# The modulation products beside the heads of three attentions, on GpSimd instead of VectorE

## The reference

```python
def ada_params(c, w, b):
    mod = jax.nn.silu(c) @ w + b
    shift, scale, gate = jnp.split(mod, 3, axis=-1)

def modulated_residual(x, c, g, w_mod, b_mod, fn):
    shift, scale, gate = ada_params(c, w_mod, b_mod)
    h = rms_norm(x, g) * (1 + scale) + shift
    return x + gate * fn(h)
```

## Time and profile before

| | |
|---|---|
| median of 3 runs | 2230.7 us (2225.03 to 2233.52) |
| profiled execution, its time | 2235.24 us |
| profiled execution, its span | 2233.4 us |
| granted TensorE clock, mean | 0.916 |
| TensorE busy | 1965.2 us, 88% |
| VectorE busy | 1664.8 us, 75% |
| ScalarE busy | 1143.7 us, 51% |
| GpSimd busy | 36.5 us, 2% |
| products L1370 | 192, 243.9 us, 1280 ns each |

### The profile page before, as it was taken

How to read it: one execution, slowest core, us unless ns; L and a number is a source line. 1 busy time by engine, 2 the same in 40 slices (tenths; PEclk the granted TensorE clock), 3 DMA queues, 4 the chain that set the end, 5 groups by cost and what they waited for, 6 DMA issues and landing times.

```text
span 2233.4 us, 29567 instructions
## 1 busy us (share of the span) xinstructions
PE 1965.2 (88%) x9224; PEld 1633.4 (73%) x9224; DVE 1664.8 (75%) x2294; ACT 1143.7 (51%) x1600; POOL 36.5 (2%) x47
## 2 busy tenths in 40 slices
PE   2968999877799999999999999585779998678998
PEld 2956887656678888888888888564768877466886
DVE  7877666967498989898898989675676668566554
ACT  2434444333277777777777777424344443434443
POOL 2000000000000000000000000000000000000000
PEclk9988999876699999999999999786689998679999
DMA  7965873964189999999999999373457866435662
GB/s 266 363 204 187 263 250 121 335 201 164 57 287 339 368 337 364 336 350 354 340 362 338 366 337 368 134 248 91 134 178 260 261 209 207 112 112 160 216 208 85
DMA packets 368358, 551.03 MB, mean 247 GB/s; under 512 B 35715, under 2 KB 292998, under 8 KB 368230
## 3 DMA queue, kind: packets, MB, share of 16 engines
q1 hardware_dynamic: 353120, 542.56, 71.9%
q10 hardware_dynamic: 14278, 6.70, 2.2%
q0 software_dynamic: 832, 0.30, 0.1%
HBM read 548.38 MB, written 1.08 MB: 246 GB/s over the span
## 4 chain that ended last, share of the span: by engine, by line
PE 75%; DVE 14%; DMA 5%; issue 3%; ACT 2%; SPq 0%; ACTq 0%; POOL 0%; DVEq 0%; POOLq 0%
PE ps L381 21%; PE ps L383 21%; PE ps L382 21%; PE ps L773 2%; DVE mod_acc L1370 2%; PE ps L919 2%; DVE units_low L376 2%; DMA raw_units<-in_w_in 1%; PE ps L827 1%; PE ps L762 1%; PE ps L750 1%; DMA raw_units<-in_attn_w_qkv 1%; DVE x_tokens L1396 1%; DMA raw_units<-in_conv_w_in 1%; DVE x_normed L1395 1%
## 5 line engine op out<-in xcount | busy, mean ns | idle before, releaser
L376 DVE TENSOR_TENSOR units_low<-raw_units,units_high 128x1024 fp32r<-128x1024 f32 (+2 forms) x840 | 983.5, 1219 | 213.1 <-ACT units_high L372 207.7
L372 ACT ACTIVATE units_high<-raw_units 128x1024 fp32r<-128x1024 f32 (+2 forms) x840 | 845.3, 1057 | 355.0 <-PE ps L383 230.4
L381 PE MATMUL ps<-units_high,hT_high 128*128 128x512 f32 (+2 forms) x1592 | 636.5, 400 | 70.4 <-DVE units_low L376 30.1
L382 PE MATMUL ps<-units_low,hT_high 128*128 128x512 f32 (+2 forms) x1592 | 631.6, 397 | 0.0
L383 PE MATMUL ps<-units_high,hT_low 128*128 128x512 f32 (+2 forms) x1592 | 631.3, 397 | 0.0
L381 PEld LDWEIGHTS ps<-units_high,hT_high 128*128 128x128 f32 (+1 forms) x1592 | 306.4, 192 | 141.0 <-issue 38.1
L383 PEld LDWEIGHTS ps<-units_high,hT_low 128*128 128x128 f32 (+1 forms) x1592 | 305.3, 192 | 67.2
L382 PEld LDWEIGHTS ps<-units_low,hT_high 128*128 128x128 f32 (+1 forms) x1592 | 306.0, 192 | 65.9
L381 PE MATMUL ps<-units_high,aT_high 128*128 128x512 f32 x616 | 252.5, 410 | 0.0
L1370 DVE SCALAR_TENSOR_TENSOR mod_acc<-mod_in,silu_c,mod_acc 128x1024 f32<-128x1024 f32 x192 | 243.9, 1280 | 6.2 <-DMA mod_in<-in_mod_w 3.2
L382 PE MATMUL ps<-units_low,aT_high 128*128 128x512 f32 x616 | 242.9, 394 | 0.0
(11 more groups left out here) (229 smaller groups left out, 1570.0 us busy)
## 6 DMA issues: line engine op xcount, KB each, us to landing
raw_units<-in_moe_w_gate SPq DMA_DIRECT2D x352, 256.0 KB, 4.4
raw_units<-in_moe_w_up SPq DMA_DIRECT2D x352, 256.0 KB, 5.6
raw_units<-in_moe_w_down SPq DMA_DIRECT2D x176, 512.0 KB, 6.1
mod_in<-in_mod_w SPq DMA_DIRECT2D x96, 512.0 KB, 5.8
mod_in<-in_w_mod SPq DMA_DIRECT2D x96, 512.0 KB, 5.5
raw_units<-in_w_gu SPq DMA_DIRECT2D x176, 256.0 KB, 3.3
raw_units<-in_w_down SPq DMA_DIRECT2D x44, 512.0 KB, 4.1
raw_units<-in_w_in SPq DMA_DIRECT2D x32, 512.0 KB, 8.5
```

The costliest lines, as they stand in the source:

```text
L372: eng.activation(whi[:rows, n % H, 0:width], raw[:rows, n % R, 0:width], ACT.Copy).then_inc(f.hi, 1)
L376: eng.tensor_tensor(low[:rows, n % R, 0:width], raw[:rows, n % R, 0:width], whi[:rows, n % H, 0:width].bitcast(F32), ALU.subtract).then_in ...
L381: pe.matmul(dst, ah, bh, start=start, stop=False, **kw)
L382: pe.matmul(dst, ah, bl, start=False, stop=False, **kw)
```

## The change

The products are taken out of `beside_heads`, and GpSimd does them: for each, `tensor_scalar` scales the piece in its slot, GpSimd waits for that on a semaphore of its own, and `tensor_tensor` adds it to `mod_acc`. They stand in GpSimd's program for m = 4, 5 and 7 between the bias row of the columns and the memset of the gate's part. VectorE skips these numbers of `MOD_ORDER`, and its first product behind each gap waits until GpSimd's are counted. SyncE's code is unchanged.

```diff
+POOL_MODS = [(4 * MOD_COLS + 3 * MOD_GATE, MOD_GATE + MOD_COLS), (5 * MOD_COLS + 5 * MOD_GATE, MOD_COLS),
+             (7 * MOD_COLS + 7 * MOD_GATE, MOD_COLS)]
...
+    s_mterm = sem("mod_term_scaled")
...
+        terms = [0]
+
+        def mods(first, count):
+
+            pool.wait_ge(s_sc, 1)
+            for q in range(first, first + count):
+                m, gate, k, third = MOD_ORDER[q]
+                if not gate and (k, third) == (0, 0):
+                    pool.wait_ge(s_bias, 16 * (m + 1))
+                if gate and k == 0:
+                    pool.wait_ge(s_gbias, 16 * (m + 1))
+                pool.wait_ge(s_min[q % MOD_SLOTS], 16 * (q // MOD_SLOTS + 1))
+                if k >= 1 or q == first:
+                    pool.wait_ge(s_mused, q if gate or q == first else q - 1)
+                acc = mod_acc[:, third * MOD_W:(third + 1) * MOD_W]
+                at = k if m < 4 else DC + k
+                term = mod_in[:, q % MOD_SLOTS, :]
+                pool.tensor_scalar(term, term, silu_c[:, at:at + 1], None, ALU.mult).then_inc(s_mterm, 1)
+                terms[0] += 1
+                pool.wait_ge(s_mterm, terms[0])
+                pool.tensor_tensor(acc, acc, term, ALU.add).then_inc(s_mused, 1)
...
         for m in range(8):
...
+            if m in (4, 5, 7):
+                mods(*POOL_MODS[(4, 5, 7).index(m)])
...
         def mods(n):
 
+            skipped = 0
+            for first, count in POOL_MODS:
+                if mod_at[0] == first and n:
+                    mod_at[0] += count
+                    skipped = 1
             for q in range(mod_at[0], mod_at[0] + n):
                 m, gate, k, third = MOD_ORDER[q]
+                if skipped and q == mod_at[0]:
+                    ve.wait_ge(s_mused, q)
...
         def beside_heads(i):
-            mods(spread(MOD_GATE + MOD_COLS, H1 + 1, i))
...
             def beside_heads(i):
-                mods(spread(MOD_COLS, H2 + 1, i))
```

## The result

Four runs of the changed kernel have a median of 2281.8 us (2280.1 to 2283.1), four of the kernel before beside them 2232.1: a ratio of 1.022, 95% interval [1.0195, 1.0245]. The change costs 50 us; 2281 was forecast. The profiled execution has a span of 2281.3 against 2233.4, so 47.9 us more.

What follows compares the result with a forecast made beforehand. With neither TensorE nor VectorE full in the second attention, the chain of waits was taken to bound the kernel. Attentions adding +20.0, +15.5 and +14.4 gave +50 us on 2230.7: 2281, own range 2255 to 2340, wider 2235 to 2350.

Steps and rivals of the forecast that it cites:

- What is given back: Products leaving VectorE in the first attention: of 70 us moved in all three, the chain gets back about 1.8.
- The bias block's share: Second and third attention: the chain's wait for bias row blocks shortens once products' transfers are over, -1.1 and -2.2 us.
- A product on GpSimd: Scaling 1.4 us, addition 1.9 and a semaphore wait, priced from memsets: 3.6 us, between bounds of 2.2 and 5.0.
- my upper bound: Every tensor passed on GpSimd costs a memset: 5.0 us a product, first batch running to 594, +148 us, 2379.
- Both kinds of VectorE instruction are held: One-source and two-source VectorE instructions within SBUF wait, equally fully, until GpSimd's instruction ends; chance 0.54.
- The holds in the heads: VectorE's 128x2 scalings, low halves and mask terms wait 0.77 us each: +6.9 first attention, +11.6 second.
- The short steps: Nine linked two-source VectorE steps behind the first attention each let one GpSimd instruction through, 1.65 us each: +14.9.
- the copies: Eight one-source 128x64 copies ahead of the second attention's transposes, taken to wait three times: +5.0 us.
- (1): Only one-source VectorE instructions are held; short steps, low halves and mask terms go free: +22, 2253 us; chance 0.20.
- (2): No VectorE instruction is held long enough to matter: -5, 2226 us, no measurable change; chance 0.12.
- (3): Early bias blocks keep TensorE at 2.4 GHz to the end of later attentions, holds absent: -21, 2210 us; chance 0.04.
- (4): GpSimd takes over 5.3 us a product; column sums end the attention, 16 us per us above; chance 0.10.

Runs made afterwards that it cites:

- the first experiment: The changed kernel with GpSimd's scalings and additions one column wide, all waits and transfers kept: 2235.2 us, ratio 1.0003 to the kernel before.
- additions alone: The changed kernel with GpSimd's scalings one column wide, so slots are added unscaled, and its additions whole: 2283.3 us, ratio 1.0201 to the kernel before.

## Why the prediction was right, and where it was not

**What is given back (1.8 us in the first attention).** Products without duration give +1 us, interval -4.5 to +5.8, for the three attentions together, where -5 was predicted: that the gain is next to nothing was right. The 5 us lie just outside the interval, yet they are what the heads of that one trace show (-3.7, -2.3, +0.6); the times can't settle it. The bias block's share (-1.1, -2.2) rested on GpSimd at 3.6 us a product and came only with products of one column (4.29 us for 5.56; one wait of 4.57 in the third attention for two of 5.46 and 5.96).

**A product on GpSimd, 3.6 us.** It took 5.3, above my upper bound of 5.0, and is the term behind the longer batches. The step that failed is pricing a tensor passed at a memset's 0.95 us: the addition with three tensors took 2.35 where 1.9 was taken, the scaling with two 2.84 where 1.4 was. The Trainium skill's figure ("GPSIMD Engine Reference", "Performance versus the Vector engine") gave an estimate of 2.25 us for the addition, and the trace agrees (2.35).

**Both kinds of VectorE instruction are held.** Right, and shown: one-source ones by writing alone, two-source ones only by an instruction that reads (0.17 us beside memsets, 2.27 beside an addition). Wrong in "as fully": a scaling frees the two-source ones after 1.1 us, and the one-column scalings were never held.

**The holds in the heads.** 6.9, 11.6 and about as much in the third attention were forecast, less what is given back 5.1, 10.5 and 9.4; the heads became 7.5, 7.5 and 8.3 us longer. The instructions in flight were longer than I took them, while scalings held less: two errors of opposite sign.

**The short steps, +14.9.** This is the step that failed most: +3.0. "Each step lets one through" took nine holds in a row; two of nine were held (2.27 and 1.05 us), and the others passed in the 1.7 us that the scaling left free.

**What made up for it.** The first batch ran to 610 us where the forecast had it end at 560, and held the residual, the norm and hT: 10.1 us that stood only in my upper bound. So the first attention's +20 was met (7.5 + 3.0 + 10.1 + 1.3 = 21.9) by other terms than mine. The second and third were forecast at +15.5 and +14.4, and came to 10.6 and 11.3; the copies took 2.3 us more, not 5.0. The mechanism was right, but that the total of 50 came within 1 us is luck: in the first attention 11.9 us too many for the short steps met 10.1 too few behind them, and in the trace the later two fell 8 us short while 5.4 came from stretches that the forecast leaves alone (3.8, 1.3 and 0.3).

**The rivals.** (1) fell with L1703's 2.27 us; (2) with the medians, 0.696 against 0.169 us; (3) with the first experiment; (4) missed by little: a product took 5.26 us undisturbed and 5.5 in the mean of the second batch, over the limit of 5.3, but the heads had become longer too, so the batch was over at 1617.7 and the heads at 1624.9; it appeared at 5.7.

## What to carry to other kernels

Before moving work off an engine, make the moved work one column wide and time that: here it gave nothing measurable (-4.5 to +5.8 us), so there was next to nothing to win by moving it. In this kernel GpSimd's instructions stopped VectorE's within SBUF, and what they cost is set by what VectorE has on the chain beside them and by how long a single one is, not by GpSimd's busy time; so keep two-source instructions there short and away from linked steps, and tiny one-source steps in single columns. Instructions on two engines that wait for each other can fall in step, and an estimate by random arrival is then low by half (0.9 us estimated, 1.75 to 2.29 measured with additions alone).

## What the runs showed of the hardware that I had not expected

- GpSimd's scaling of 128x1024 fp32 in place with a pointer scalar takes 2.84 us, more than the addition of two such tensors (2.35) and three times a memset (0.95).
- A scaling holds VectorE's two-source instructions for its first 1.1 us only; an addition of 2.34 us holds them to the end, if they begin inside it.
- VectorE's 128x1 fp32 scaling is not held by an addition in flight (0.153 to 0.155 us in all 47), its 128x2 one is (up to 2.29).
- The hold goes both ways: the one that begins first isn't held. In the changed kernel an addition took 3.36 us that began 0.06 us behind a low half, and the low half its usual 1.22; a scaling of 2.84 us took 4.87 beside two low halves. Timelines of GpSimd and VectorE:

```profile
500.99 3.36 POOL L556 TENSOR_TENSOR mod_acc<-mod_acc,mod_in 128x1024 f32<-128x1024 f32 x1
...
563.84 4.87 POOL L553 TENSOR_SCALAR mod_in<-mod_in,silu_c 128x1024 f32<-128x1024 f32 x1
```

```profile
500.93 1.22 DVE L381 TENSOR_TENSOR units_low<-raw_units,units_high 96x1024 fp32r<-96x1024 f32 x1 [6.07 <-ACT units_high L377]
...
561.51 4.57 DVE L381 TENSOR_TENSOR units_low<-raw_units,units_high 96x1024 fp32r<-96x1024 f32 x2 [0.81 <-ACT units_high L377]
567.00 1.22 DVE L381 TENSOR_TENSOR units_low<-raw_units,units_high 96x1024 fp32r<-96x1024 f32 x1 [0.92 <-ACT units_high L377]
```

What stays open: whether the arrival in step is why the addition alone costs as much as both together (it is read from the 18 holds of one trace, and was not varied by itself), what it is in a scaling's first and last microsecond that holds VectorE, and whether other numbers of columns than one go free.
